# Score products of the prompt attention as three rounded matmuls in place of one plain fp32 matmul

## The reference, cut to what matters

```python
s = jnp.einsum('btkgd,bnkd->bkgtn', qg, cmp_kv[:, :, 0]) - slopes * d_c
p_cmp = masked_softmax(s, d_c >= 0)
...
s = jnp.einsum('btkgd,bktmd->bkgtm', qg, ksel) - slopes * d_s
...
s = jnp.einsum('btkgd,bskd->bkgts', qg, win_kv[:, :, 0]) - slopes * d_w
o = g[:, :, 0] * o_cmp + g[:, :, 1] * o_slc + g[:, :, 2] * o_win
```

## Time and profile before

| | us |
|---|---|
| median of three runs | 1778.66 |
| profiled execution | 1777.28 |
| its span, first to last instruction | 1775.6 |
| TensorE busy | 1725.7 (97%) |
| VectorE busy | 1214.2 (68%) |
| GpSimd busy | 839.6 (47%) |
| ScalarE busy | 802.9 (45%) |

### The profile page before, as it was taken

How to read it: one execution, slowest core, us unless ns; L and a number is a source line. 1 busy time by engine, 2 the same in 40 slices (tenths; PEclk the granted TensorE clock), 3 DMA queues, 4 the chain that set the end, 5 groups by cost and what they waited for, 6 DMA issues and landing times.

```text
span 1775.6 us, 35974 instructions
## 1 busy us (share of the span) xinstructions
PE 1725.7 (97%) x13587; PEld 1601.2 (90%) x13587; DVE 1214.2 (68%) x1813; ACT 802.9 (45%) x1458; POOL 839.6 (47%) x862
## 2 busy tenths in 40 slices
PE   8999999999989999999998999999999999999998
PEld 7999999999966667666998899999999999999998
DVE  6789974779777677767557655454597979755435
ACT  5312233565866666667435233333434333324335
POOL 2203954555524343434544655656665545326521
PEclk9999998999999999999999999999999999999999
DMA  5421356665432443442414322223493742331114
GB/s 161 129 70 42 96 172 160 176 155 135 142 96 84 141 135 101 129 135 68 146 33 143 113 105 101 105 97 110 145 307 105 218 142 89 137 124 57 48 36 146
DMA packets 179724, 214.62 MB, mean 121 GB/s; under 512 B 22941, under 2 KB 150665, under 8 KB 174800
## 3 DMA queue, kind: packets, MB, share of 16 engines
q1 hardware_dynamic: 174461, 196.82, 36.1%
q0 software_dynamic: 4032, 13.40, 2.6%
q10 hardware_dynamic: 1058, 2.10, 0.4%
HBM read 181.30 MB, written 35.59 MB: 122 GB/s over the span
## 4 chain that ended last, share of the span: by engine, by line
PE 56%; DVE 8%; issue 3%; POOL 2%; ACT 2%; DMA 0%; ACTq 0%; SPq 0%; DVEq 0%; POOLq 0%
PE ps L2756 12%; PE ps L3139 7%; PE ps L2761 6%; PE ps L2516 5%; PE ps L3144 4%; PE ps L200 3%; PE ps L1923 3%; PE ps L3652 3%; PE ps L1911 3%; PE ps L1935 3%; POOL S L1878 2%; PE ps L1962 2%; DVE S L2172 2%; PE ps L206 2%; PE ps L3662 1%
## 5 line engine op out<-in xcount | busy, mean ns | idle before, releaser
L1878 POOL TENSOR_SCALAR S<-S,inv,gate_p 128x640 f32<-128x640 f32 (+7 forms) x186 | 125.0, 690 | 193.6 <-DVE inv L2182 193.6
L1275 DVE SCALAR_TENSOR_TENSOR y<-u,conv_w,y 128x1024 f32<-128x1024 f32 x120 | 156.0, 1347 | 1.2
L3139 PE MATMUL ps<-dn_op_hi,dn_hi 128*128 128x264 f32 x672 | 136.6, 285 | 2.9 <-DVE dn_op_lo L3187 2.9
L3139 PE MATMUL ps<-dn_op_lo,dn_hi 128*128 128x264 f32 x672 | 135.7, 283 | 0.0
L645 POOL COPY relaid<-raw 128x512 f32<-128x512 f32 x128 | 83.8, 685 | 90.3 <-PE ps_p L1050 45.9
L2059 ACT ACTIVATE S<-S,mn 128x64 f32<-128x64 f32 (+8 forms) x180 | 108.7, 608 | 2.1 <-DVE mn L2172 2.1
L3070 POOL TENSOR_TENSOR dn_lo<-dn_t_sum,dn_hi 128x512 fp32r<-128x512 f32 x48 | 76.1, 1585 | 66.9 <-ACT dn_hi L3092 66.7
L2756 PE MATMUL ps<-s_hi,up_hi 128*128 128x264 f32 x512 | 104.6, 286 | 3.0 <-ACT rstd L2726 3.0
L3139 PEld LDWEIGHTS ps<-dn_op_hi,dn_hi 128*128 128x128 f32 x672 | 103.7, 188 | 4.1 <-DVE dn_op_lo L3187 4.1
L979 PE MATMUL ps_p<-Ahi,win_hi 128*128 128x352 f32 x456 | 103.8, 327 | 1.5 <-DVE Alo L1252 1.5
L2756 PE MATMUL ps<-s_lo,up_hi 128*128 128x264 f32 x512 | 104.2, 285 | 0.0
(11 more groups left out here) (492 smaller groups left out, 5095.9 us busy)
## 6 DMA issues: line engine op xcount, KB each, us to landing
s_raw<-in_cache_slc_kv_dram SPq DMA_DIRECT2D x256, 128.0 KB, 2.1
raw<-in_cache_cmp_kv_dram SPq DMA_DIRECT2D x192, 128.0 KB, 3.8
dn_op_raw<-hidden SPq DMA_DIRECT2D x21, 1056.0 KB, 6.0
hidden<-cs SPq DMA_DIRECT2D x32, 528.0 KB, 2.6
up_raw<-in_w_up_dram SPq DMA_DIRECT2D x16, 1024.0 KB, 5.5
dn_w<-in_w_down_dram SPq DMA_DIRECT2D x48, 256.0 KB, 5.2
win_raw<-in_w_in_dram SPq DMA_DIRECT2D x38, 256.0 KB, 3.3
raw<-in_cache_cmp_kv_dram POOLq DMA_DIRECT2D x64, 128.0 KB, 3.7
```

The lines of the kernel that those rows point to most:

```text
L1275: i = V_.scalar_tensor_tensor(out=y, in0=x, scalar=w, in1=y, op0=ALU.mult, op1=ALU.add)
L1878: nc.gpsimd.tensor_scalar(x, x, inv[:, n % 3, 3 * e + br:3 * e + br + 1], c.gate_p[:, i, H * br + h:H * br + h + 1], ALU.mult, ALU.mult).t ...
L3139: nc.tensor.matmul(ps[:, 2 * m + j, 0:HC], w_hi[q % 4][:, k, :], x[:, k, HC * j:HC * j + HC], start=(k == 0 and x is op_hi[n]), stop=False)
```

## The change

Keys and queries are split. `K_hi`, `KcP_hi` and `q_hi` are rounded copies by ScalarE; `K_lo`, `KcP_lo` and `q_lo` the differences by VectorE. `qk` then issues for each piece high x high, high query x low key, and low query x high key, both heads in each, into the same PSUM columns. The keys (1024 columns, selected and window together) are split once, in two parts cut at column 384, before the stage's first step. The first query is split there too. The others follow in the units' work: ScalarE rounds the query of unit n+3 first in unit n, VectorE computes its low part last in unit n's first step, and the first chunk of unit n+3 waits for it. `K_hi` takes room in which two ring slots lay, so the ring has four slots. With that, SyncE waits for other quads before it fills a slot, before it loads the output weights (`slot_free`), and ScalarE before the second part of `y_hi`.

```diff
-RAW_PLACE = (AREA + 8192, RAW_OFF, HIY_OFF, HIY_OFF + 8192, AREA)
+RAW_SLOTS = 4
+RAW_PLACE = (HIY_OFF, RAW_OFF, HIY_OFF + 8192, AREA + 8192)
+KEY_CUT = 384
...
+    query_part = lambda n: 1 if n == 2 else n + 2
+    KEY_PARTS = (slice(0, KEY_CUT), slice(KEY_CUT, T))
...
-            if h >= 5:
-                sp.wait_ge(t_done, turn_no["o", (h - 5) // 2] + 1)
+            if h >= RAW_SLOTS:
+                sp.wait_ge(t_done, turn_no["o", (h - RAW_SLOTS) // 2] + 1)
...
+            if ch == 0:
+                pe.wait_ge(part_lo, 3 if n == 2 else query_part(n))
+            w0 = P * max(0, i - 4)
+            hi, lo = q_hi[n % 2], q_lo[query(n)]
...
-                    mm = nc.tensor.matmul(ps_S[:, s + e, off:off + w], c.q[rows, g, P * i:P * i + P], keys, start=True, stop=True)
...
+                for m, (x, split, compressed) in enumerate(((hi, K_hi, KcP_hi), (hi, K_lo, KcP_lo), (lo, K_hi, KcP_hi))):
+                    for e in range(KVH):
+                        rows = slice(DH * e, DH * e + DH)
+                        mm = nc.tensor.matmul(ps_S[:, s + e, off:off + w], x[rows, :], keys(rows, split, compressed), start=(m == 0), stop=(m == 2))
...
+        def query_high(n):
+            if n >= 4:
+                act.wait_ge(qk_done, score_no["p", n - 2, len(CHUNKS[n - 2]) - 1] + 1 - len(EARLY))
+            nc.scalar.activation(q_hi[n % 2][:], c.q[query(n)], ACT.Copy).then_inc(part_hi, 1)
+
+        query_high(2)
+        nc.scalar.activation(K_hi[:, :, KEY_PARTS[0]], c.proj[:, KS:KW + 1, KEY_PARTS[0]], ACT.Copy).then_inc(part_hi, 1)
+        nc.scalar.activation(KcP_hi[:], c.KcP[:], ACT.Copy).then_inc(part_hi, 1)
+        nc.scalar.activation(K_hi[:, :, KEY_PARTS[1]], c.proj[:, KS:KW + 1, KEY_PARTS[1]], ACT.Copy).then_inc(part_hi, 1)
...
+                if j == 0 and n + 3 < NU:
+                    query_high(n + 3)
                 for k in steps[st]:
...
-                    if k == 0:
-                        act.wait_ge(t_done, turn_no["o", NZ - 2] + 1)
+                    if k < 2:
+                        act.wait_ge(t_done, turn_no["o", NZ - 2 + k] + 1)
...
+        def query_low(n):
+            dve.wait_ge(part_hi, query_part(n))
+            V_.tensor_tensor(q_lo[query(n)], c.q[query(n)], q_hi[n % 2][:].bitcast(F32), ALU.subtract).then_inc(part_lo, 1)
...
                     first_scores(gr)
+                if j == 0 and n + 3 < NU:
+                    query_low(n + 3)
...
-    c.t_done, c.slot_free = t_done, turn_no["o", NZ - 3] + 1
+    c.t_done, c.slot_free = t_done, turn_no["o", NZ - 2] + 1
```

More of the change, by code:

```diff
@@ L1673, in attend @@
     LOW = 1e20
-    raw = [c.at(f"s_raw{s}", [P, 8, 256], F32, RAW_PLACE[s]) for s in range(5)]
+    raw = [c.at(f"s_raw{s}", [P, 8, 256], F32, RAW_PLACE[s]) for s in range(RAW_SLOTS)]
+    K_hi = c.at("K_hi", [P, 2, T], F32R, AREA)
+    K_lo = c.at("K_lo", [P, 2, R], F32R, PROJ_OFF + 4 * R * KS)
+    KcP_hi = c.at("KcP_hi", [P, 64], F32R, RSTD_OFF + 4096)
+    KcP_lo = c.at("KcP_lo", [P, 64], F32R, B1_OFF + 15616)
+    q_lo = c.at("q_lo", [P, PAIRS, R], F32R, U_OFF)
     KT_ = [c.at(f"s_KT{s}", [P, QK_], F32, PT_OFF + 8192 + 2048 * s) for s in range(4)]
@@ L1809, in attend @@
     HALF_DMAS = lambda h: 2 if place(h // 2) == 0 else 8
-    arrived = lambda h: 16 * sum(HALF_DMAS(x) for x in range(h % 5, h + 1, 5))
+    arrived = lambda h: 16 * sum(HALF_DMAS(x) for x in range(h % RAW_SLOTS, h + 1, RAW_SLOTS))
     qk_done, score_read = c.sem("qk_done"), c.sem("score_read")
@@ L1816, in attend, with query @@
     iotas, step = c.sem("s_iotas"), c.sem("s_dve_step")
-    raw_loaded = [c.sem(f"s_raw_loaded{s}") for s in range(5)]
+    raw_loaded = [c.sem(f"s_raw_loaded{s}") for s in range(RAW_SLOTS)]
+    part_hi, part_lo = c.sem("key_or_query_hi_ready"), c.sem("key_or_query_lo_ready")
+    query_part = lambda n: 1 if n == 2 else n + 2
+    KEY_PARTS = (slice(0, KEY_CUT), slice(KEY_CUT, T))
+    def query(n):
+        g, i = UNITS[n]
+        return (slice(None), g, slice(P * i, P * i + P))
     cmp_ready, cmp_exp, imp_ready, selected = c.sem("s_cmp_max"), c.sem("s_cmp_exp"), c.sem("s_imp_ready"), c.sem("s_selected")
@@ L1826, in page @@
     def page(h, bb, j):
[L1828 removed]
+        return raw[h % RAW_SLOTS][:, 4 * (bb % 2) + j, :]
     def on_sp(sp):
@@ L1842, in on_sp @@
                     for j in range(4):
-                        sp.dma_start(page(h, bb, j), cache[ds(pages[j], 1)].rearrange("o t f -> (o t) f")).then_inc(raw_loaded[h % 5], 16)
+                        sp.dma_start(page(h, bb, j), cache[ds(pages[j], 1)].rearrange("o t f -> (o t) f")).then_inc(raw_loaded[h % RAW_SLOTS], 16)
     def on_pool(pool):
@@ L1905, in qk, with keys @@
             off = 0
+            if ch == 0:
+                pe.wait_ge(part_lo, 3 if n == 2 else query_part(n))
+            w0 = P * max(0, i - 4)
+            hi, lo = q_hi[n % 2], q_lo[query(n)]
             for br, k0, w in CHUNKS[n][ch]:
[L1907 to L1911 removed]
+                def keys(rows, split, compressed):
+                    return compressed[rows, :] if br == 0 else split[rows, 0, k0:k0 + w] if br == 1 else split[rows, 1, w0 + k0:w0 + k0 + w]
+                for m, (x, split, compressed) in enumerate(((hi, K_hi, KcP_hi), (hi, K_lo, KcP_lo), (lo, K_hi, KcP_hi))):
+                    for e in range(KVH):
+                        rows = slice(DH * e, DH * e + DH)
+                        mm = nc.tensor.matmul(ps_S[:, s + e, off:off + w], x[rows, :], keys(rows, split, compressed), start=(m == 0), stop=(m == 2))
                 off += w
```

17 lines of the change are left out of this document (10 added, 7 removed).

## The result

The changed kernel takes 1781.5 us (median of 20 runs, 1776.3 to 1786.1) where the kernel before takes 1778.3 beside it (20 runs, 1776.6 to 1780.0). The ratio is 1.0015, 95% interval 1.0008 to 1.0021: 1.4 to 3.7 us slower, 2.7 at the middle. Predicted were 1779.4, a ratio of 1.0004. Here the changed kernel's runs also lie wider apart, by 9.7 against 3.4 us, but in other sets of 21 to 35 runs the kernel before spreads over 5 to 6.

A forecast was written before the change was run, and what follows sets the result against it. TensorE, busy 324.8 of 346 us, was taken as nearly full. Terms -3.1 + 1.2 + 1.0 + 1.6 = +0.7 us on the profiled 1777.3 gave 1778.0, as median 1779.4; range 1771 to 1790.

The forecast's parts named there:

- three rounded products: TensorE's score products: three rounded rounds for two plain ones save 4.3 us of TensorE, -3.1 us on the path.
- query's parts, waits of one-step units: 29 more query splits on ScalarE and VectorE: +1.0 us by chain shares, +1.6 for four waits at one-step units.
- four slots: Page ring with four slots instead of five: loads stay hidden with 2.3 us to spare, price 0.
- start of the stage: Roundings and differences ahead of the first score products: first product 0.8 us late, VectorE's scores later, +1.2 us.
- path share of 0.71: Chain of work in the stretch: of each microsecond saved on TensorE, 0.71 counts on the path.
- lower bound: Score products without the 0.012 us extra a round and with weight loads of 0.107 us: -7.0 us of TensorE.
- the two queues: Rival: the query parts added on ScalarE and VectorE end on the path, half of 16.2 us counting; 1786.5 us, chance 0.17.
- upper bound of 2.9: Start of the stage, if ScalarE's first copies were wanted at once: its five roundings sum to 2.9 us.
- full gain: Rival: TensorE saves 7.0 us, all on the path, extra work in idle time, only the start's 1.2 paid; 1772.9 us, chance 0.20.
- heads one after the other: Rival: the two heads' rounded matmuls run in turn, six a piece, +53 us on TensorE; 1835 us, chance 0.06.
- loads shown: Rival: no round's weight load hides behind the round before, 70 more loads of 0.11 us; 1784.9 us, chance 0.06.
- Narrow pieces at the slow rate: Rival: narrow rounded matmuls cost the plain product's four cycles a column, adding 6.8 us; 1784.2 us, chance 0.06.

The follow-up runs named there:

- plain product: Changed kernel with all parts still made and waited for, but each piece one plain fp32 product of the high parts: 1785.9 us, ratio 1.0037 to the kernel before.
- ring alone: Kernel before with four page slots instead of five, their places and waits, nothing else: 1778.3 us beside 1779.7, ratio 1.0001.
- The one before it: Changed kernel with units 2 and 3 multiplied plainly and the keys' parts made later on ScalarE and VectorE: 1781.7 us, ratio 1.0011 to the kernel before.

## Why the prediction was near, and which term was not

The range of 1771 to 1790 us was easy to hit: every kernel of this study lies between 1778 and 1786. The terms say more. Against the first profile of the kernel before, the profiles give each its size:

| term | predicted us | measured us | from |
|---|---|---|---|
| three rounded products | -3.1 | -3.2 | later units, changed kernel against plain product |
| query's parts, waits of one-step units | +2.6 | +2.1 | later units, without them |
| four slots | 0 | +0.2 | ring alone, later units (as far apart as two profiles of one kernel) |
| start of the stage | +1.2 | +2.8 | windows up to unit 2's output (32.77 against 29.97) |
| sum | +0.7 | +1.9 | stage 343.78 against 341.88 |

Against the second profile of the kernel before, which has no stretch of lower clock in unit 2, the start costs 4.3 and the sum is 3.4. The 2.7 us of the runs lie between the two sums.

*The product.* Right in its rounds and in its sum, though two small errors cancel in the sum: less was saved than the 4.3 us, and more of it reached the end. A round of 512 columns is 0.23 us where I took 0.225, chunks of one wide and one narrow piece take 0.88 and 0.45 where I said 0.88 and 0.47, and TensorE's busy time in the later units fell by 3.8. The path share of 0.71, read from the chain, gave -3.1; taking the product back costs 3.2 of 4.1, a share of 0.78. No load is shown between rounds: the second row at 575.73 is 0.33 behind the first, the third 0.23 behind it, with 0.213 for one cycle a column. The 0.107 for a load in the lower bound stands in no row; narrow rounds are 0.11 to 0.13 apart. The Trainium skill, "TensorE: Matmul & The Clock Gate", Part 3: Packing small matmuls, would have a load overlap a matmul only in another row group; the trace disagrees, since each head's loads are for the row group in which its matmul is running, and the rounds cost 0.02 us more than their columns.

*The query's parts.* Near in the sum, with luck in the waits. The wait at unit 8 is the 0.40 us that was forecast there (row at 614.73). Four such waits were to make 1.6 us; there are three, 0.27, 0.40 and 0.89, which make 1.56, and the longest comes from GpSimd's addition beside the subtraction, which I did not price. ScalarE's copy, of which the rival of the two queues was afraid, became no bound at all: 0.2 us of waits. Some 0.4 us of this term is an order that I did not price either: the low part stands between the last scores and the reciprocal for which GpSimd waits.

*The pages.* Near in the time, but not free. I said none and 2.3 us to spare; TensorE waits for pages for 0 to 1.0 us in the profiles with four slots, and not at all in the two with five. The slack was reckoned too small besides, since seven steps in 5.36 us plus one are 6.1 us and not 7. So the mean slack of the rows said nothing of the late transfers.

*The start of the stage.* Here the prediction is off, by 1.6 us (3.1 against the second profile of the kernel before): the largest error of the sum. Against the first profile it is inside the upper bound of 2.9, but that bound was ScalarE's five roundings, another reason. Its own instants were right: I put the first product 0.8 us late and it came 0.9 late, the first scores 1.2 and they came 0.8. The step that failed is the sentence "So +1.2": that a delay at the first scores is the delay of what follows. Behind it stood three things. The clock stayed low for 3.2 us longer, which is 0.8 on the sampled scores. That TensorE's idle time there kept it low is argued and not shown: with that time filled it still rose only after 6.3 us, and in the kernel with the first two units plain after 6.4. The low part of the second query held up TensorE by 0.27 and the reciprocal by 0.2. And with GpSimd 2.0 us late the next fall of the clock met a chunk of wide products, 1.36 us. The kernel with the keys' low parts on GpSimd takes all three away together, and its window has 18.09 us: the loss belongs to the order of the work at the start. The one before it shows that the first product's place alone isn't enough: there GpSimd was late for another reason, and the loss was the same. How the 2.8 us divide among the three I can say for this one profile only; where the clock's stretches fall differs from execution to execution, and no experiment held it fixed. That the changed kernel's runs lie wider apart fits with that and was not tested.

*GpSimd beside VectorE.* Not in the prediction at all. I priced VectorE's subtractions for VectorE's queue and for TensorE, and not for GpSimd, which scaled unit 1 beside them: 4.88 us instead of 2.92. That was nearly harmless there (0.2 us of the stage came back when a part of it was taken away), and cost 1.4 us where the scaling was wanted. The Trainium skill, "SBUF — State Buffer", Who interferes with whom, states that a VectorE instruction with two SBUF inputs contends with a GpSimd instruction that reads SBUF; the trace agrees, with the 4.98 us against 3.58.

The rivals: full gain is out, since the product's saving is 4 us and not 7; the two queues are out at 2.1 us for what they put at 8.1; heads one after the other and loads shown are out by the rows at 575.40; the second of them was priced too low, at one load a piece where no hidden load means three. Narrow pieces at the slow rate are out by the rounds of 128 columns, 0.11 us apart (567.81 and 567.92) and not 0.213.

## What to carry to other kernels

A change that makes TensorE's work smaller by splitting operands is priced by what makes the parts: here the product gave back 3.2 us and its parts cost 2.1 along the way and 2.8 or more at the start. Put the making of parts where the engine beside it is idle, not only where the engine that makes them is; ask of each two-input operation on VectorE what GpSimd does meanwhile, and what that does to either. And when a delay stands at the start of a stage, follow it to the next wait of TensorE and look at the granted clock there before calling it a constant.
